# Storing the moving operands of the dense products backwards, and reading them backwards

## The reference

```python
# first block, for each of 2 layers (h is 512 x 1024)
proj  = h @ w_in[l]                                   # 1024 -> 2594
mixed = concatenate([nsa_mixer(..), gla_mixer(..), pool_mixer(..)])
h  = layer_norm(ALPHA * h + mixed @ w_out[l], ln1_g[l], ln1_b[l])
ff = square(relu(h @ w_up[l])) @ w_down[l]            # 1024 -> 4096 -> 1024
h  = layer_norm(ALPHA * h + ff, ln2_g[l], ln2_b[l])

# second block, for each of 2 layers
h = h + 0.5 * rms_norm(swiglu(rms_norm(h, g[0]), ffn_wi[i, 0], ffn_wo[i, 0]), g[1])  # 1024 -> 2 x 2816 -> 1024
y = mixer(rms_norm(h, g[2]), ...)                     # dilated in layer 0, windowed in layer 1
h = h + rms_norm(y, g[3])
h = h + 0.5 * rms_norm(swiglu(rms_norm(h, g[4]), ffn_wi[i, 1], ffn_wo[i, 1]), g[5])
e = p[i] @ ple_proj[i]
gate = sigmoid(rms_norm(h, g[6]) @ ple_gate[i])
h = h + rms_norm(e * gate, g[7])
```

## Time and profile before

| what | value |
|---|---|
| median of three runs | 3432.22 us |
| profiled execution, its own time | 3430.66 us |
| its span, first to last instruction | 3428.8 us |
| TensorE busy | 3317.4 us, 97% of the span |
| VectorE, ScalarE, GpSimd busy | 1836.8, 1241.6, 342.3 us |
| mean granted clock of TensorE | 0.988 of full speed |
| read from HBM | 296.14 MB, 87 GB/s over the span |

### The profile page before, as it was taken

One profiled execution on the slowest core, in us unless ns is written; L12 is line 12 of the kernel. 1 busy time (PEld: TensorE's weight loads), 2 busy tenths in 40 slices (PEclk: granted clock), 3 DMA queues, 4 the chain that ended last, 5 costly groups with the idle time before them and its releaser, 6 DMA issues.

```text
span 3428.8 us, 42531 instructions
## 1 busy us (share of the span) xinstructions
PE 3317.4 (97%) x16570; PEld 2633.9 (77%) x16570; DVE 1836.8 (54%) x2932; ACT 1241.6 (36%) x1878; POOL 342.3 (10%) x244
## 2 busy tenths in 40 slices
PE   9999999999899999999999999999999989999997
PEld 6667888776688887888777778887788876688886
DVE  5776334567752446443566664435644357654436
ACT  3354222424442324332333342324432235532324
POOL 0310000212100020000233100000000012100001
PEclk9999999999999999999999999999999999999999
DMA  4102222311122222223322122232222321122232
GB/s 162 62 32 74 96 95 98 128 62 50 50 85 94 98 98 81 98 97 104 107 74 68 63 81 96 98 105 93 86 96 94 105 94 39 61 98 98 98 105 80
DMA packets 81431, 300.35 MB, mean 88 GB/s; under 512 B 9040, under 2 KB 9040, under 8 KB 80640
## 3 DMA queue, kind: packets, MB, share of 16 engines
q1 hardware_dynamic: 78624, 284.20, 24.8%
q0 software_dynamic: 1568, 11.98, 0.9%
q10 hardware_dynamic: 1088, 2.10, 0.2%
HBM read 296.14 MB, written 2.10 MB: 87 GB/s over the span
## 4 chain that ended last, share of the span: by engine, by line
PE 88%; DVE 6%; ACT 3%; issue 1%; POOL 1%; DMA 1%; ACTq 0%; DVEq 0%; POOLq 0%
PE bank L874 25%; PE bank L876 25%; PE bank L875 24%; PE bank L918 2%; PE bank L925 2%; PE bank L919 2%; DVE wl L2026 1%; PE bank L1411 1%; ACT sc L1710 1%; PE bank L1423 1%; PE bank L1175 1%; PE bank L1156 1%; ACT wh L1549 1%; PE bank L1466 1%; PE bank L1114 1%
## 5 line engine op out<-in xcount | busy, mean ns | idle before, releaser
L874 PE MATMUL bank<-x,wh 128*128 128x512 f32 x2632 | 1053.7, 400 | 14.8 <-DVE h L2470 5.7
L876 PE MATMUL bank<-x,wl 128*128 128x512 f32 x2632 | 1027.3, 390 | 0.0
L875 PE MATMUL bank<-x,wh 128*128 128x512 f32 x2632 | 1026.1, 390 | 0.0
L1549 ACT ACTIVATE wh<-raw 128x1024 fp32r<-128x1024 f32 x528 | 558.0, 1057 | 1171.6 <-PE bank L876 1083.6
L2026 DVE TENSOR_TENSOR wl<-raw,wh 128x1024 fp32r<-128x1024 f32 x528 | 677.7, 1284 | 567.4 <-ACT wh L1549 566.0
L874 PEld LDWEIGHTS bank<-x,wh 128*128 128x128 f32 x2632 | 494.9, 188 | 135.9 <-issue 29.4
L876 PEld LDWEIGHTS bank<-x,wl 128*128 128x128 f32 x2632 | 494.6, 188 | 105.4
L875 PEld LDWEIGHTS bank<-x,wh 128*128 128x128 f32 x2632 | 495.7, 188 | 98.4 <-issue 3.4
L874 PE MATMUL bank<-mid,wh 128*128 128x512 f32 x1216 | 474.9, 391 | 0.5 <-DVE wl L2026 0.5
L876 PE MATMUL bank<-mid,wl 128*128 128x512 f32 x1216 | 473.1, 389 | 0.0
L875 PE MATMUL bank<-mid,wh 128*128 128x512 f32 x1216 | 473.1, 389 | 0.0
(11 more groups left out here) (340 smaller groups left out, 3294.5 us busy)
## 6 DMA issues: line engine op xcount, KB each, us to landing
raw<-stream SPq DMA_DIRECT2D x528, 512.0 KB, 3.3
raw_apart<-stream SPq DMA_DIRECT2D x10, 512.0 KB, 3.6
sm<-small POOLq DMA_DIRECT2D x2, 2144.0 KB, 10.6
tb<-tab POOLq DMA_DIRECT2D x2, 1728.0 KB, 14.8
h<-x_t ACTq DMA_DIRECT2D x4, 512.0 KB, 6.8
out_t<-h SPq DMA_DIRECT2D x8, 256.0 KB, 2.1
tba<-tab_a POOLq DMA_DIRECT2D x1, 1152.0 KB, 8.5
pf<-p_t POOLq DMA_DIRECT2D x2, 512.0 KB, 3.9
```

The lines of the kernel that those rows point to most:

```text
L874: pe.matmul(dst, hi, src[:, kc, 0, :], start=start, stop=False)
L875: pe.matmul(dst, hi, src[:, kc, 1, :], start=False, stop=False)
L876: return pe.matmul(dst, lo, src[:, kc, 0, :], start=False, stop=stop)
L1549: act.activation(high_of(n)[:, :], raw_of(n)[:, :], ACT.Copy).then_inc(hi_done, 1)
```

## The change

All 26 changed statements put `::-1` on the token axis of an access pattern, in three kinds. TensorE's moving operand is read from the last token to the first; where a chunk is written straight into `x`, `px`, `ao` or `bo`, its writer writes from the last place to the first (and VectorE reads the high part so, too); where it goes through `prod` into `mid`, the scratch tile is read backwards and `mid` is written forwards. The results in PSUM keep their order of tokens. Sizes, buffers, waits and the order of the instructions on every engine stay as they were.

```diff
@@ piece, reads x, mid, ao, bo, px
-                pe.matmul(dst, hi, src[:, kc, 0, :], start=start, stop=False)
-                pe.matmul(dst, hi, src[:, kc, 1, :], start=False, stop=False)
-                return pe.matmul(dst, lo, src[:, kc, 0, :], start=False, stop=stop)
+                pe.matmul(dst, hi, src[:, kc, 0, ::-1], start=start, stop=False)
+                pe.matmul(dst, hi, src[:, kc, 1, ::-1], start=False, stop=False)
+                return pe.matmul(dst, lo, src[:, kc, 0, ::-1], start=False, stop=stop)
@@ abreast, reads x
-                pe.matmul(dst, hi, x[:, kc, 0, :], start=kc == 0, stop=False)
-                pe.matmul(dst, lo, x[:, kc, 0, :], start=False, stop=False)
+                pe.matmul(dst, hi, x[:, kc, 0, ::-1], start=kc == 0, stop=False)
+                pe.matmul(dst, lo, x[:, kc, 0, ::-1], start=False, stop=False)
...
-                    mm = pe.matmul(dst, hi, x[:, kc, 1, :], start=False, stop=kc == 7)
+                    mm = pe.matmul(dst, hi, x[:, kc, 1, ::-1], start=False, stop=kc == 7)
@@ ScalarE, high part of x after an RMS norm (the other writers of x, px, ao, bo alike)
-                act.activation(x[:, k, 0, :], h[:, k, :], ACT.Copy, scale=vec[:, g + k:g + k + 1]).then_inc(x_hi, 1)
+                act.activation(x[:, k, 0, ::-1], h[:, k, :], ACT.Copy, scale=vec[:, g + k:g + k + 1]).then_inc(x_hi, 1)
@@ ScalarE, high part of mid (both feed-forward forms)
-                        act.activation(mid[:, i * 4 + k, 0, :], prod[k % 2][:, :], ACT.Copy).then_inc(mid_hi, 1)
+                        act.activation(mid[:, i * 4 + k, 0, :], prod[k % 2][:, ::-1], ACT.Copy).then_inc(mid_hi, 1)
@@ VectorE, low part of x after an RMS norm
-                dve.scalar_tensor_tensor(x[:, k, 1, :], h[:, k, :], vec[:, g + k:g + k + 1],
-                                         x[:, k, 0, :].bitcast(F32), ALU.mult, ALU.subtract).then_inc(x_ready, 1)
+                dve.scalar_tensor_tensor(x[:, k, 1, ::-1], h[:, k, :], vec[:, g + k:g + k + 1],
+                                         x[:, k, 0, ::-1].bitcast(F32), ALU.mult, ALU.subtract).then_inc(x_ready, 1)
@@ VectorE, low part of mid (both feed-forward forms)
-                        lo_of(mid[:, i * 4 + k, 1, :], prod[k % 2][:, :], mid[:, i * 4 + k, 0, :], mid_ready)
+                        lo_of(mid[:, i * 4 + k, 1, :], prod[k % 2][:, ::-1], mid[:, i * 4 + k, 0, :], mid_ready)
@@ mixer outputs, dilated mixer (reorders the tokens as well)
-                        out_hi(ungrouped(ao[:, k, 0, :]), grouped_src(bank[7][:, :]), k)
+                        out_hi(ungrouped(ao[:, k, 0, ::-1]), grouped_src(bank[7][:, :]), k)
```

More of the change, by code:

```diff
@@ L1588, in layer_norm @@
                     if to_x:
-                        act.activation(x[:, k, 0, :], prod[k % 2][:, :], ACT.Identity, bias=bias).then_inc(x_hi, 1)
+                        act.activation(x[:, k, 0, ::-1], prod[k % 2][:, :], ACT.Identity, bias=bias).then_inc(x_hi, 1)
                         c.tick("affine")
@@ L1671, in _ @@
                     act.wait_ge(h_in[k // 2], 16)
-                act.activation(x[:, k, 0, :], h[:, k, :], ACT.Copy).then_inc(x_hi, 1)
+                act.activation(x[:, k, 0, ::-1], h[:, k, :], ACT.Copy).then_inc(x_hi, 1)
             split(2)
@@ L1769, in _ @@
                         ch = (GO, GO + 1, GO + 2, PU, PU + 1)[k]
-                        act.activation(x[:, 3 + k, 0, :], proj[:, ch, :], ACT.Copy).then_inc(mx_hi, 1)
+                        act.activation(x[:, 3 + k, 0, ::-1], proj[:, ch, :], ACT.Copy).then_inc(mx_hi, 1)
                     elif stage == "exps":
@@ L1780, in _ @@
                         act.wait_ge(o_done, 12 * layer + 4 * k + 4)
-                        act.activation(x[:, k, 0, :], bank[7][:, :], ACT.Copy).then_inc(ot_hi, 1)
+                        act.activation(x[:, k, 0, ::-1], bank[7][:, :], ACT.Copy).then_inc(ot_hi, 1)
                 c.tick("shifted", DC)
@@ L1849, in two @@
                         c.wait(pair_made)
-                        act.activation(mid[:, i * 2 + k, 0, :], prod[k][:, :], ACT.Copy).then_inc(mid_hi, 1)
+                        act.activation(mid[:, i * 2 + k, 0, :], prod[k][:, ::-1], ACT.Copy).then_inc(mid_hi, 1)
                 c.start(banks_gated)
@@ L1860, in ffn2 @@
                     for k in range(2):
-                        act.activation(px[:, k, 0, :], pf[:, k, :], ACT.Copy).then_inc(p_hi, 1)
+                        act.activation(px[:, k, 0, ::-1], pf[:, k, :], ACT.Copy).then_inc(p_hi, 1)
                     c.wait(p_ready, 2)
@@ L1952, in mixer_b @@
                     elif stage == "out":
-                        out_hi(bo[:, k, 0, :], bank[7][:, :], 4 + k)
+                        out_hi(bo[:, k, 0, ::-1], bank[7][:, :], 4 + k)
                 rest(4)
@@ L2070, in layer_norm @@
                         c.wait(x_hi)
-                        dve.scalar_tensor_tensor(x[:, k, 1, :], prod[k % 2][:, :], vec[:, g + 8 + k:g + 9 + k],
-                                                 x[:, k, 0, :].bitcast(F32), ALU.add, ALU.subtract).then_inc(x_ready, 1)
+                        dve.scalar_tensor_tensor(x[:, k, 1, ::-1], prod[k % 2][:, :], vec[:, g + 8 + k:g + 9 + k],
+                                                 x[:, k, 0, ::-1].bitcast(F32), ALU.add, ALU.subtract).then_inc(x_ready, 1)
                         c.tick("made x_ready")
@@ L2367, in _ @@
                 c.wait(x_hi)
-                lo_of(x[:, k, 1, :], h[:, k, :], x[:, k, 0, :], x_ready)
+                lo_of(x[:, k, 1, ::-1], h[:, k, :], x[:, k, 0, ::-1], x_ready)
             split(2)
@@ L2429, in _ @@
                         c.wait(mx_hi)
-                        lo_of(x[:, 3 + k, 1, :], proj[:, ch, :], x[:, 3 + k, 0, :], x_ready)
+                        lo_of(x[:, 3 + k, 1, ::-1], proj[:, ch, :], x[:, 3 + k, 0, ::-1], x_ready)
                     elif stage == "values_in":
@@ L2449, in _ @@
                         c.wait(ot_hi)
-                        dve.tensor_tensor(x[:, k, 1, :], bank[7][:, :], x[:, k, 0, :].bitcast(F32),
+                        dve.tensor_tensor(x[:, k, 1, ::-1], bank[7][:, :], x[:, k, 0, ::-1].bitcast(F32),
                                           ALU.subtract).then_inc(ot_ready, 1)
@@ L2531, in two @@
                         c.wait(mid_hi)
-                        lo_of(mid[:, i * 2 + k, 1, :], prod[k][:, :], mid[:, i * 2 + k, 0, :], mid_ready)
+                        lo_of(mid[:, i * 2 + k, 1, :], prod[k][:, ::-1], mid[:, i * 2 + k, 0, :], mid_ready)
                 c.start(banks_gated)
@@ L2541, in ffn2 @@
                         c.wait(p_hi)
-                        lo_of(px[:, k, 1, :], pf[:, k, :], px[:, k, 0, :], p_ready)
+                        lo_of(px[:, k, 1, ::-1], pf[:, k, :], px[:, k, 0, ::-1], p_ready)
                 for k in range(DC):
@@ L2649, in mixer_a @@
                     elif stage == "out_lo":
-                        out_low(ungrouped(ao[:, k, 1, :]), grouped_src(bank[7][:, :]), ungrouped(ao[:, k, 0, :]), k)
+                        out_low(ungrouped(ao[:, k, 1, ::-1]), grouped_src(bank[7][:, :]), ungrouped(ao[:, k, 0, ::-1]), k)
                 rest(1)
@@ L2697, in mixer_b @@
                     elif stage == "out_lo":
-                        out_low(bo[:, k, 1, :], bank[7][:, :], bo[:, k, 0, :], 4 + k)
+                        out_low(bo[:, k, 1, ::-1], bank[7][:, :], bo[:, k, 0, ::-1], 4 + k)
                 rest(4)
```

## The result

| | before | after |
|---|---|---|
| median of the runs (4 each) | 3431.67 us | 3501.22 us |
| lowest to highest | 3431.01 to 3433.68 us | 3500.12 to 3503.73 us |
| span of the profiled execution | 3428.8 us | 3499.1 us |
| TensorE busy | 3317.4 us | 3391.4 us |

The ratio is 1.0203 (95% interval 1.0185 to 1.022): 70 us slower, outside the range of the prediction. The span grew by 70.3 us, TensorE's busy time by 74.0 us, and its idle time fell by 3.7 us.

What follows compares the result with a forecast made beforehand. TensorE was taken as the bound, through its matmuls' count and distance. The profiled 3430.66 us + 0 for TensorE's read + 0 for the writers, with the median 1.56 us above, gave 3432.2 us; range 3424 to 3468 us.

Steps and rivals of the forecast that it cites:

- What bounds the kernel, the count of matmuls, their distance: Whole kernel: TensorE bounds it, with 12720 matmuls 0.2266 us apart, 2882 us or 84% of the span.
- the sign that the prediction had named: Feed-forward and other matmuls: the reasoning would be wrong if distances on `x` and on `mid` differed from one another.
- TensorE's read: Moving operand of 12720 matmuls, read falling: nothing lost taken, between a gain of 169 us and 8700 us more.
- VectorE's strided copy: `xp<-proj`, reading SBUF at a step of 16 elements: 1096 ns for 992 elements, used as TensorE's upper bound.
- The third rival: Every matmul: a fixed cost up or down, bounded by 0.0133 us each; 3601 us, or 3263 us as gain; chance 0.05.
- The first rival: TensorE's matmuls: a falling operand read at half pace, 0.4267 us each, about 5977 us; chance 0.14.
- The second rival: ScalarE's and VectorE's backward instructions: 375 ns more each, TensorE no slower; 3439 us, at most 3468 us; chance 0.12.
- the choice of "no change" for ScalarE and VectorE: Writers of the chunks: backward operands add nothing, against an upper end of 375 ns per instruction.
- the two cases that I could price: The range took in the forecast of no change, 3432.2 us, and slower writers up to 3468 us.
- the rest in the distance: Each matmul at full clock: 0.0133 us beyond columns at the array's clock; 169 us over 12720 matmuls.

Runs made afterwards that it cites:

- e3: Kernel before, TensorE reading 16-byte pieces in rising order but the 4 elements within each piece in falling order: 3430.55 us.
- e14: Kernel before, TensorE taking 16-byte pieces in turn from the lower and the upper half of a row, both rising: 3699.57 us.
- e4: Kernel before, TensorE reading the upper 256 elements in rising order, then the lower 256 in rising order: 3431.63 us.
- e6: Kernel before, read forward, with 384 columns instead of 512 in the second and third matmul of `piece`: 3116.68 us.
- e7: Changed kernel, read backward, with 384 columns instead of 512 in the second and third matmul of `piece`: 3140.07 us.
- e9: Kernel before, TensorE reading the first 16-byte piece of each row 128 times over: 3301.70 us.
- e12: Kernel before, the stationary operand of every dense product being its first weight column 128 times over: 3474.81 us.

## Why the prediction was wrong

- **What bounds the kernel, the count of matmuls, their distance:** right. 12720 x 6.7 ns = 85 us would be the loss if every matmul had shown the quiet stretch's difference; TensorE's busy time grew by 74.0 us, 5.8 ns each. Over all gapless distances at the full clock (about 12000 in each trace) the mean went from 0.2272 to 0.2334 us, 6.2 ns, which makes about these 74 us: before, about one matmul in eleven on `x` already took more than 0.229 us. The matmuls at the 1.2 GHz level, which lost nothing, are only 111. 3.7 us came back as shorter idle times. By the sign that the prediction had named, the distances on `x` (0.2334 us) and on `mid` (0.2333 us) stayed alike.
- **TensorE's read, the step that failed:** "I take nothing lost." The reason given, that a step of -1 keeps all neighbours together, is true within 16 bytes (e3) and worthless beyond them: from one piece to the next the order counts, and at the full clock 13 cycles of each matmul already went into fetches. I had seen these cycles, 0.0133 us that are "something other than columns at the array's clock", and used them as the size of a rival with a chance of 0.05 instead of asking what they were. A read that already doesn't keep up with the array has no cover for a worse order; where the columns take twice as long, at 0.427 us per matmul, every order was covered. That was the row to weigh highest; VectorE's strided copy said nothing about it.
- **The third rival** named the form of the loss, a few nanoseconds on every matmul alike, and the measured 6.7 ns lie under its bound of 13.3 ns. That was luck: 13.3 ns is what a better read could have given back, and no limit to what a worse one costs (e14: 23.3 ns more than rising). Its 3601 us took that bound as the price. The cause that it gave as an example, a start at the other end of a line, is out (e3, e4). The attention's small matmuls kept their length, as this rival had said (277 and 278 ns on line 1411). That the cost is fixed per matmul was not shown (e6, e7).
- **The first rival** (half pace) is out: 0.2333 us, not 0.4267 us. **The second rival** is out: the writers' durations stayed within 1 ns, so the choice of "no change" for ScalarE and VectorE was right.
- The note on cachelines of the Trainium skill, SBUF — State Buffer, held for what happens inside a line (e3). But at least two hits per line are not enough here: the rising read has four hits on each and still pays 13 cycles. The same note says that each access that crosses to a new line pays a penalty, which the prediction left aside; e9, which stays in one line, agrees with that. Yet every order that reads the whole row enters 128 lines, and the distance ran from 0.2267 to 0.2500 us, so the number of lines does not give the price.
- The range was drawn from the two cases that I could price and left out the one between them, though the rest in the distance, 169 us in all, was in my own working.

What stays open: which part of the chip makes the order of pieces cost. Shown is that it is a matter of the order in which TensorE takes pieces of 16 bytes, not of the place in memory at 64 or 256 bytes' shift, and not of a single step back; and that in the forward kernel the addresses of the weights count as well (e12). Whether banks of SBUF or a fetch ahead lie behind it was not told apart.

## What to carry to other kernels

Where matmuls follow each other without a gap at full clock, compare their distance with columns / 2.4 GHz; if it is longer, the read of the moving operand may be what sets the pace, and then keep that read rising and contiguous. Reversed order within 16 bytes, or in ScalarE's and VectorE's operands of 4 bytes, was free; orders that leave the rising row every 16 or 64 bytes cost each matmul 2 to 10% here. A small unexplained rest in the term that is multiplied 12720 times deserves its own question before anything else.

## What the hardware showed that I had not expected

- A 128x128x512 matmul in fp32r takes 5% longer in the best order that was tried than with a read that stays in one piece: 0.2267 us against 0.2158 us, 130 us of this kernel's 3432 us.
- Reading 64 bytes over and over (0.2419 us) costs more than reading 2048 bytes once (0.2267 us) or 256 bytes over and over (0.2267 us).
- The addresses of the weights count for the speed of the matmul beside them: all columns from one place made the kernel 44 us slower, not faster.
- With 384 columns in two of three matmuls the backward read cost these under 1 ns, and they took 0.178 us, 18 ns more than 384 columns at 2.4 GHz.
- At the 1.2 GHz level every order of the read took 0.427 us: what costs 10% at the full clock (e14) is free there.
